# A two-layer recurrent decoder trunk: where the gate part of the modulation is made

## The reference, cut to what matters

```python
mod = silu(c) @ ada_w + ada_b                  # (9, 3072) per layer, ada_w is (1024, 3072)
shift, scale, gate = split(mod, 3)
h = rms_norm(x, norm_g) * (1 + scale) + shift
proj = h @ w_in                                # branches A, B, C, D and the merge gates
up = branches @ w_up                           # four branches, 256 -> 1024 each
merged = sum(sigmoid(gl) * up over branches)
out = merged @ w_out
x_new = x + gate * out
```

## Time and profile before

| | |
|---|---|
| time, median of 3 runs | 1371.32 us (1370.52 to 1371.35) |
| the profiled execution's own time | 1368.49 us |
| its span | 1366.6 us |
| TensorE (PE) busy | 1318.0 us, 96% of the span |
| mean granted TensorE clock | 0.987 of full |
| VectorE, ScalarE, GpSimd busy | 623.3, 450.7, 375.0 us |
| bytes moved by DMA | 162.59 MB, mean 119 GB/s |

### The profile page before, as it was taken

How to read it: one execution, slowest core, us unless ns; L and a number is a source line. 1 busy time by engine, 2 the same in 40 slices (tenths; PEclk the granted TensorE clock), 3 DMA queues, 4 the chain that set the end, 5 groups by cost and what they waited for, 6 DMA issues and landing times.

```text
span 1366.6 us, 39992 instructions
## 1 busy us (share of the span) xinstructions
PE 1318.0 (96%) x18150; PEld 1190.6 (87%) x18150; DVE 623.3 (46%) x1166; ACT 450.7 (33%) x742; POOL 375.0 (27%) x286
## 2 busy tenths in 40 slices
PE   5899999999999999999989999999999999999996
PEld 4799999889899999887779999999988899988796
DVE  3557524317234336756252961332643242565643
ACT  3334422234322235231243353222442223532223
POOL 0244422223222232220333452212331222322121
PEclk9899999999999999999999999999999999999998
DMA  9833231216331272578853433212373224545932
GB/s 309 265 89 93 68 93 49 65 49 138 106 86 49 65 141 78 159 195 260 286 170 79 106 78 82 62 35 70 76 165 96 52 57 92 126 133 134 290 120 94
DMA packets 275932, 162.59 MB, mean 119 GB/s; under 512 B 86102, under 2 KB 244922, under 8 KB 275252
## 3 DMA queue, kind: packets, MB, share of 16 engines
q1 hardware_dynamic: 275220, 159.00, 42.6%
q10 hardware_dynamic: 544, 1.05, 0.2%
HBM read 135.25 MB, written 24.89 MB: 117 GB/s over the span
## 4 chain that ended last, share of the span: by engine, by line
PE 90%; DMA 3%; DVE 2%; ACT 2%; SPq 2%; issue 1%; ACTq 0%; DVEq 0%
PE psA L942 40%; PE psA L950 20%; PE psA L992 8%; PE psB L884 2%; PE psB L868 2%; DMA ring<-in_ada_w 2%; PE psB L888 1%; PE psB L1073 1%; PE psB L315 1%; PE psB L1083 1%; DMA ring<-in_w_in 1%; SPq L400 1%; PE psB L852 1%; PE psB L1311 1%; PE psB L800 1%
## 5 line engine op out<-in xcount | busy, mean ns | idle before, releaser
L778 POOL TENSOR_TENSOR w_lo<-ring,w_hi 128x512 fp32r<-128x512 f32 x248 | 331.1, 1356 | 823.6 <-ACT w_hi L1607 779.1
L942 PE MATMUL psA<-h_hi,w_hi 128*128 128x260 f32 x1984 | 426.8, 297 | 10.4 <-DVE h_lo L2034 9.4
L942 PE MATMUL psA<-h_lo,w_hi 128*128 128x260 f32 x1984 | 401.9, 284 | 0.8 <-issue 0.8
L942 PEld LDWEIGHTS psA<-h_hi,w_hi 128*128 128x128 f32 x1984 | 307.4, 190 | 30.4 <-issue 19.1
L942 PEld LDWEIGHTS psA<-h_lo,w_hi 128*128 128x128 f32 x1984 | 308.7, 190 | 1.4 <-issue 1.1
L950 PE MATMUL psA<-h_hi,w_lo 128*128 128x260 f32 x1984 | 273.6, 286 | 0.0
L950 PEld LDWEIGHTS psA<-h_hi,w_lo 128*128 128x128 f32 x1984 | 249.0, 187 | 6.8 <-issue 3.0
L1607 ACT CAST w_hi<-ring 128x1024 fp32r<-128x1024 f32 x120 | 123.9, 1032 | 10.0 <-DMA ring<-in_w_in 9.9
L893 ACT COPY ws<-psB 128x128 f32<-128x128 f32 x80 | 21.4, 268 | 190.0 <-PE psB L868 162.6
L1637 ACT ACTIVATE tg<-psA 128x520 f32<-128x520 f32 x48 | 28.9, 602 | 119.5 <-PE psA L950 119.3
L901 DVE COPY_PREDICATED tg<-tmask,psB 128x128 f32<-128x128 uint8 x40 | 14.2, 355 | 102.6 <-PE psB L888 58.9
(11 more groups left out here) (504 smaller groups left out, 1973.3 us busy)
## 6 DMA issues: line engine op xcount, KB each, us to landing
ring<-in_w_in SPq DMA_DIRECT2D x122, 512.0 KB, 4.3
ring<-in_ada_w SPq DMA_DIRECT2D x32, 512.0 KB, 5.9
scr_tanh<-tg SPq DMA_DIRECT2D x48, 260.0 KB, 4.6
upw<-in_w_up SPq DMA_DIRECT2D x64, 128.0 KB, 3.5
RB<-in_w_out SPq DMA_DIRECT2D x16, 512.0 KB, 3.8
RA<-scr_tanh SPq DMA_DIRECT2D x30, 260.0 KB, 3.8
ws<-scr_tanh SPq DMA_DIRECT2D x24, 260.0 KB, 4.2
xT<-scr_x SPq DMA_DIRECT2D x8, 520.0 KB, 4.7
```

The costliest lines, as they stand in the source:

```text
L778: nc.gpsimd.tensor_tensor(tile_part(RL[s][:, k], (kind, n)), tile_part(RS[s][:, k], (kind, n)), tile_part(HS[L.hslot[q]][:, k], (kind, n)) ...
L942: nc.tensor.matmul(out(h), HS[L.hslot[q]][:, p, 0:m], cols(part(p), h), start=(p == 0 and part is hi), stop=False)
```

## The change

The pieces of the gate leave the stretch of up tiles in both layers.

- **Layer 0's gate.** SyncE loads its 8 pieces in the head of layer 0 into `RB` (`load_first_gate`): four behind the load of projection tile 4, four behind projection tile 5. TensorE takes them behind projection tiles 4 and 7, and `mod_columns` behind tile 8; VectorE makes the gate (`gate_modulation`) before it takes projection tile 9.
- **Layer 1's gate.** SyncE loads its 8 pieces in layer 0 (`load_late`): two behind up tile 13, three behind output tile 4, three behind output tile 5, into parts of `ws`, `RC`, `RB` and `RA`. TensorE takes two before and six behind the sum of squares that ends layer 0, and `mod_columns` behind projection tiles 0 and 1 of layer 1.
- **The head of layer 0** is in another order: the last block of the prologue's `ada_w` is loaded before the weights of projection tile 1, ScalarE splits these weights only behind `mod_rows0(act, 3)`, and TensorE runs projection tile 0 alone over the first half before `ada0(pe, 3)`. The low parts of projection tiles 0 and 1 stand between the second halves, in layer 1 too.
- **Small DMAs** move: the state loads stand two ring loads later, the stores of last rows and the load of layer 1's parameters come with output tiles 2 and 3, and layer 1's first state load waits for the last late piece.

```diff
-                self.up_piece = {k: m for m, k in enumerate((20, 22, 24, 26, 28, 29, 30, 31))}
+                tail = [("up", k) for k in range(18, 32)]
...
+        LATE = [two(t, at) for t, at in ((ws, 10), (RC, 2), (RB, 6), (ws, 0), (RC, 0), (RB, 4), (RA, 2), (ws, 16))]
+        FIRST_GATE = [two(RB, 2 * (m % 4)) for m in range(8)]
...
             ada_loads(1)
+            ada_loads(3)
             first_load(sp, 1, LAYERS[0], 0)
-            ada_loads(3)
...
             first_split(act, 0, LAYERS[0])
-            first_split(act, 1, LAYERS[0])
...
+                    if layer == 0 and x == ("proj", 5):
+                        sp.wait_ge(*pe_f.at("ada", 3))
+                        load_first_gate(4, 5, 6, 7)
+                    if layer == 0 and x == ("up", 13):
+                        sp.wait_ge(*dn.at("gated", 2))
+                        load_late(0, 1)
+                    if layer == 0 and x == ("out", 4):
+                        sp.wait_ge(*dn.at("gated", 3))
+                        sp.wait_ge(*merged_at(31))
+                        load_late(2, 3, 4)
+                    if layer == 0 and x == ("out", 5):
+                        load_late(5, 6, 7)
...
-                for p in range(KT):
-                    if layer == 0 and p == KT // 2:
-                        ada0(pe, 3)
-                        mod0(pe, 2)
-                        mod0(pe, 3)
+                if layer == 0:
+                    proj(0, range(KT // 2))
+                    ada0(pe, 3)
+                    mod0(pe, 2)
+                    mod0(pe, 3)
+                    proj(0, (KT, KT + 1))
+                    proj(1, range(KT // 2))
+                    proj(1, (KT, KT + 1))
+                for p in range(KT // 2 if layer == 0 else 0, KT):
+                    for idx in range(2):
+                        proj(idx, [p])
+                    if p % 2:
                         for idx in range(2):
-                            proj(idx, (KT, KT + 1))
-                    proj(0, [p])
-                    proj(1, [p])
-                for idx in range(2):
-                    proj(idx, range(KT + 2 if layer == 0 else KT, PARTS))
+                            proj(idx, [KT + p // 2])
+                if layer:
+                    for b in range(2):
+                        pe.wait_ge(*LAYERS[0].TR["act_f"].at("modrow", 6 + b))
+                    for b in range(2):
+                        mod_columns(late_mods, b, modrow[:, b, :]).then_inc(*LAYERS[0].TR["pe_f"].step("mod"))
                 for idx in range(2, P_D):
                     proj(idx)
+                    if layer == 0 and idx in (4, 7):
+                        b = (4, 7).index(idx)
+                        for kp in range(4):
+                            pe.wait_ge(s_first[4 * b + kp], 16)
+                            ada_products(first_gate_bank(b), wide(FIRST_GATE[4 * b + kp]), 2 * kp, kp == 0, kp == 3).then_inc(*pe_f.step("ada"))
...
                 for idx in range(18, 32):
                     up(idx)
-                    if idx in L.up_piece:
-                        ada(L.up_piece[idx])
...
                 if layer == 0:
+                    late(0)
+                    late(1)
                     square_sums().then_inc(*pe_f.step("ss"))
+                    for m in range(2, 8):
+                        late(m)
```

More of the change, by code:

```diff
@@ L701, in before @@
                         decode_vectors(2)
-                    elif (kind, n) == ("ada", 2):
+                    elif (kind, n) == ("out", 2):
                         if layer == 0:
@@ L717, in _ @@
                     sp.wait_ge(*pe0.at("mod", 3))
+                else:
+                    sp.wait_ge(*LAYERS[0].TR["pe_f"].at("ada", 31))
                 sp.dma_start(srow[:, :], a["state_rows"][layer]).then_inc(s_st, 16)
@@ L1023, in _ @@
                 pe.wait_ge(*ap.at("proj", 9))
+                if layer:
+                    pe.wait_ge(*LAYERS[0].TR["dve_f"].at("gate", 1))
                 crow_rows([RA[:, j] for j in range(7)], 0, 0, pa.step("crow"))
@@ L1029, in _ @@
                 pe.wait_ge(s_w2, 16 * N_W2)
+                if layer == 0:
+                    pe.wait_ge(*dve_f.at("gate", 0))
                 for g in range(2):
@@ L1573, in _ @@
                         ada(n)
-                    if layer and e == 0:
-                        mods(1)
                     if layer == 0 and e == 6:
@@ L1683, in _ @@
                     A(hhi[:, d, 0:SEQ], hT[:, d, 0:SEQ], ACT.Identity, bias=modT[:, d, 8:9]).then_inc(*act_f.step("hh"))
+                if layer:
+                    for b in range(2):
+                        act.wait_ge(*LAYERS[0].TR["pe_f"].at("mod", 4 + b))
+                        act.wait_ge(*LAYERS[0].TR["pe_f"].at("ada", 27 + 4 * b))
+                        nc.scalar.copy(modrow[:, b, :], late_bank(b)).then_inc(*LAYERS[0].TR["act_f"].step("modrow"))
                 evac(0, 1)
@@ L2069, in _, with gate_modulation @@
                 S_(der[:, 14:16], der[:, 30:32], -LRU_C / 2, None, mult)
+                def gate_modulation(bank, last_mod):
+                    f0 = LAYERS[0].TR
+                    dve.wait_ge(*f0["pe_f"].at("mod", last_mod))
+                    did(f0["dve_f"], "modT", T_(modT[:, 16:24, :], bank[:, 0:72].rearrange("p (r s) -> p r s", r=8), bc(par("ada_b", 16, 8), 2, 9), add), layer)
+                    did(f0["dve_f"], "gate", S_(modT[:, 16:24, :], modT[:, 16:24, :], 0.5, None, mult), layer)
+                if layer:
+                    gate_modulation(late_mods, 7)
                 dve.wait_ge(*pe_f.at("st"))
```

78 lines of the change are left out of this document (54 added, 24 removed).

## The result

The changed kernel takes 1362.97 us in the median of 12 runs (1354.0 to 1367.13), the kernel before 1370.67 us in 12 runs beside it (1368.02 to 1373.74): ratio 0.9942, 95% interval 0.9927 to 0.9957, some 8 us. Measured a second time, beside its own runs of the kernel before, it gave 1364.61 against 1369.23, ratio 0.9971 (0.9955 to 0.9987), 4 to 5 us; two of those 29 runs of the kernel before (1443.59 and 3472.67 us) are in a slow state and left out of its median. Forecast were 1361.1, in a range of 1355.5 to 1366.0, and a gain of 10.2 us.

A forecast was written before the change was run, and what follows sets the result against it. The prediction took TensorE, on the chain for 90% of the span, as the bound. Its terms, -5.4 - 5.5 + 5.5 - 6.2 - 0.95 + 3.0 - 0.65, sum to -10.2 us: median 1371.3 becomes 1361.1, range 1355.5 to 1366.

The forecast's parts named there:

- Price of a piece, pieces in the head (+5.5): Layer 0's head: a piece costs 0.56 us, so 8 pieces and two `mod_columns` add 5.5 us, with no cover.
- Up tiles (-5.4 and -5.5): The 14 up tiles without gate pieces: 5.4 us less in layer 0 (27.5 us), 5.5 less in layer 1 (27.0).
- The rival that weights bound the tiles: Up tiles: weight landings stay at 3.7 to 4.5 us, waits of 1.9 and more a layer, 1364 to 1366 us; 12%.
- The head's order (-6.2): Layer 0's head: new order brings modulation 4.8 us sooner and starts projection tile 2 at 52.2, 6.2 us sooner in all.
- The 1.0 us for low parts in the gaps: Layer 0's head: 8 of 16 low records fill the steps of DVE between second-half rows, saving 1.0 us.
- the 0.9 for a clock that stays up: Layer 0's head: with fewer gaps TensorE should not fall to the lower clock, saving 0.9 us.
- Late loads ahead of pieces 22 and 23 (+3.0): Layer 0's output tiles: three late loads queued first make piece 22 wait 2.1 us and piece 23 0.8 more, +3.0 us.
- Between the layers (-0.65): End of layer 0 to layer 1's head: six pieces free, two +0.1, low parts -2.0, `mod_columns` +0.95, split +0.3: -0.65 us.
- The 2.0 us for interleaved low parts: Layer 1's head: low records standing in the gaps between high ones save 2.0 us, between 0.5 and 2.8.
- Late loads were not free: Judges the rival that late loads cost nothing, pieces 22 and 23 landing in time and clock holding: 1356 to 1358 us; 14%.
- that rival's 1 to 3 us: Rival that layer 0's head gives little, late data or another wait: 3 to 5 us worse than forecast, 1364 to 1366; 10%.
- the slower case: Rival: late and weight loads hold the stores of `x`, for which layer 1's `h_hi` waits: 1374 to 1378 us; 4%.

The follow-up runs named there:

- experiment 7: Experiment 5's both-layers kernel, GpSimd's subtractions for tile 1's low weights (layer 0's head) held until VectorE's last `h_lo`: second only 1357.18 us, both (first-half low parts also moved) 1355.96.
- experiment 5: Experiment 1's kernel with low parts of tiles 0 and 1 back behind all high parts: in layer 1 only 1359.35 us, in both layers 1358.01 us.
- experiment 1: Changed kernel with the first three of the six late loads queued behind gate pieces 22 and 23 instead of ahead: 1360.16 us, ratio 0.9934.
- low parts last in layer 1: Experiment 1's kernel with the low parts of tiles 0 and 1 back behind all high parts in layer 1's head only: 1359.35 us, ratio 0.9925.
- experiment 6: Experiment 5's both-layers kernel with 128 more waits, on a semaphore long reached, in TensorE's program at layer 0's start: 1364.25 us, ratio 0.9963.

## Why the prediction was right, step by step

The time was right, the gain was not so near: 10.2 us were forecast, the medians give 7.7 and 4.6. That the time came out within 2 us is in part luck: the up tiles and the pieces were mis-sized to the safe side, by 3 us in all, and made up for half of what failed: the head's order, the low parts between the layers, and the clock behind the late loads.

- **Price of a piece, pieces in the head (+5.5).** Right, with no cover there as said. Tile 2 to tile 10 is 5.0 us longer with them, so a piece costs some 0.49 us there, not 0.56.
- **Up tiles (-5.4 and -5.5).** Right in kind and too small: -6.4 and -7.1. The terms were mis-sized. The waits for weights came to 0.4 us in layer 0 where 0.7 were taken, and to none in layer 1 where 0.4 were. And 0.3 us for VectorE weren't needed at all; in layer 1 tiles run at 1.81 us with TensorE never idle. The rival that weights bound the tiles is out: wherever the pieces are gone, in nine profiles of layer 0 and eight of layer 1, the 14 tiles take 25.3 to 26.8 us, with no wait for weights over 1.21 us. The fixed cost of 2.0 us that the prediction takes from the Trainium skill, DMA: Bandwidth & Descriptors, Anatomy of one DMA, is given there for DMAs issued by GpSimd. These loads are issued by SyncE, so the measured 6.4 and 7.1 us beside its 6.5 are no test of that figure.
- **The head's order (-6.2).** The step that failed. Its first part was even better than forecast, modulation 6.35 us sooner instead of 4.8 (and the working gives less than 4.8: data at 38.7 and 3.2 us behind it are 41.9, 4.3 sooner, not the 41.3 to 41.5 that it names). What was missed is that the moved split of tile 1's weights sends GpSimd's subtraction into VectorE's chain for the second half: 2.1 us, shown in experiment 7. The 1.0 us for low parts in the gaps didn't come either (experiment 5), nor the 0.9 for a clock that stays up: the fall came again, and went only in experiment 7, where it gave the 1.0 us that it was priced at. The 0.5 us for the split of tile 2 was right (a wait of 1.25 us instead of 0.77). Against the earlier trace rows the whole gives 4.0 instead of 6.2 us.
- **Late loads ahead of pieces 22 and 23 (+3.0).** Right in kind, by the mechanism named, the queue's order: the two waits are 3.2 us. Mis-sized by the clock, which fell behind the wait: against the kernel of experiment 1 the stretch is longer by 2.0 us beyond the waits, 1.2 of it in output tile 6, so that the whole is 5.2 us there, and 4.4 by layer 1's first projection.
- **Between the layers (-0.65).** The pieces are free there, as said. The 2.0 us for interleaved low parts failed; measured is +1.0 for the head of layer 1, all of it `mod_columns`.
- **The rivals.** Late loads were not free (3.2 us and a fall of the clock), the head gave less than forecast but more than that rival's 1 to 3 us, and the slower case did not come: layer 1's first `h_hi` follows VectorE's `hT`, with no wait for a store in front of it. That case is near, though: in four of the six kernels with the three loads behind the pieces (experiment 1, low parts last in layer 1, and both of experiment 7) the same `h_hi` does wait for the store of `x`, and from the end of the output tiles to layer 1's first projection it is 8.7 to 10.0 us in the six, 8.4 in the changed kernel.
- **The rest of the layers (0).** Here the profiles differ by 2.7 us (7.7 less the 5.0 of the pieces) and 4.0. The clock's falls and the gaps make most of it, and it differs between two profiles of one kernel by 2.6 and 3.6 us. It is also why the profiled execution shows 1.3 us of a gain of some 8. Layer 1's stage takes 546.9 to 548.9 us in the three profiles without late pieces and 548.2 to 555.1 in the eight with them, so 1 or 2 us may belong to the change after all, by where it puts the gaps; experiment 6, with the gaps elsewhere, has the 548.2. That stays open.
- **The sum.** With the measured stages, and 5.0 us for the pieces in the head: -4.0 + 5.0 - 6.4 + 3.2 + 1.2 + 1.0 - 7.1 - 1.0 = -8.1 us, beside 7.7 and 4.6 in the medians of the two measurements.

How much the clock makes of a run's time, whole runs show: among the changed kernel's first 12 runs the fastest (1354.0 us) had a mean clock of 0.995, the two slowest 0.987 and 0.988 (1365.33 and 1367.13). What decides whether a fall happens at a given place stays open.

## What to carry to other kernels

A transfer that is needed late goes behind one that is needed soon, even if its buffer is free earlier: three loads of 512 KB ahead of two pieces cost 5 us here, and changing the place of one call gave 4.4 of them back. When a step is moved forward in time, look at what its followers on other engines then run beside: the cost was not on ScalarE, where the split was moved, but on VectorE, which GpSimd's subtraction of the same tile held up, and on TensorE's clock, which stayed up only once the wait had become short. And where an untouched stage of hundreds of us varies by more than the change is worth, compare kernels stage by stage, from matmul to matmul, and take the sum from medians of many runs.

## What the runs showed that was not expected

- TensorE stops for 0.2 to 1.5 us with nothing that releases it, at places that come back in front of the same matmul and, within one stretch, 254 to 256 matmuls or about a multiple of it apart; most are in stretches of small matmuls (some 20 per us). 128 extra waits took them away from where they were. Gaps of 0.17 us and more sum to 3.8 and 3.1 us in the two profiles of the changed kernel and to 1.8 us in the one before.
- A wait on a semaphore that has long been reached is not free on TensorE: 128 of them took 5.14 us, 0.04 us each, where the expectation had taken 0.03 at most.
- The hold of VectorE by GpSimd stands in the kernel before too, between the layers: its 128x64 operation at L2043 (705.05) takes 0.88 us beside subtractions that start at 703.36 and 704.58, and 0.88 to 0.92 in all eleven profiles, where another 128x64 operation with two inputs (L2041, 701.93) takes 0.22. No run here moves that subtraction, so what it would give is not shown.
